# Out-projection begun with three of four head pairs, and roundings reordered around the turned rows, in a two-block transformer kernel

## The chip, the cores and the metric

One core of one Trainium2 chip runs the whole program. The metric is the device time of one execution in microseconds; lower is better. TensorE is called PE here, ScalarE ACT, VectorE DVE, GpSimd POOL and SyncE SP, as in the profile.

## The reference

The input is 256 tokens of width 1024 in float32. Two blocks of two layers each are computed one after the other.

First block, per layer: `h = rms_norm(x)`; `z = h @ w_in` (2560 columns); three mixers read z; their outputs are concatenated and `x = x + mix @ w_out`; then an MLP.

```
o_att = block_attention(rope(norm(q_a)), rope(norm(k_a)), v_a)      # 8 heads of 64, 2 kv heads
o_hg  = hgrn2_bidirectional(...)                                   # 4 heads, gated recurrence both ways
o_cv  = silu(layer_norm(depthwise_conv(a * sigmoid(gate)) + b_dw)) # 256 channels, 31 taps
x = x + concat([o_att, o_hg, o_cv]) @ w_out
x = x + square(relu(rms_norm(x) @ w_mlp_in)) @ w_mlp_out
```

Second block: layer 0 is a gated linear attention, layer 1 a dilated attention of 3 groups and 6 slots over shared keys; both have 4 more heads over an outside memory. Then `x = layer_norm(alpha * x + mix @ w_out)` and `x = layer_norm(alpha * x + peer(x))`, where `peer` picks 16 of 16384 experts for each of 8 heads and is computed densely, with a table of gates.

## The kernel before, in words

**Products in three parts.** Every float32 operand of a large product is split into a high part, rounded to the format fp32r, and a low part, the rest. One product is three matmuls (L1630, L1631, L1632 in `three`): high x high, low x high, high x low. The weights come as 403 panels of 128 x 2048 (1 MB) in one stream. SP loads a panel into one of 4 slots `RAW`; ACT rounds it (`hi`, L468); DVE subtracts (`lo`, L992), POOL for a few of them; PE multiplies. `hi_to(n)` and `lo_to(n)` do this for all panels up to n, so the place of such a call in ACT's or DVE's program sets what stands behind the rounding. The semaphores are `raw_loaded`, `hi_ready`, `lo_ready` and `hp_used` (PE is done with the panel). SP reloads a slot on `lo_ready`. A panel's result is in one of four PSUM banks `PS` (lin in the trace); the reader frees it through `bank_free`. The other four banks are `M`.

**Order.** Each engine runs its own list of instructions, written out by hand; they meet only in semaphores.

**Start.** ACT loads constants, `LBS` (lower bounds) and `PR` (parameters). DVE waits for all three (`cst_loaded` at 48), shifts `LBS` (L1037 to L1039), ACT takes the exponential (L511), DVE finishes (L1041 to L1051). Only behind L511 does ACT take the squares of the rows of x in `rms_rows` (L503); DVE scales the rows (`norm_rows`, L1021); PE turns them (`transposes`, L1617). Ahead of the turns PE runs copies of constants into a bank that nobody reads (`warm`, L1607): 11 at the start, 2 at later norms. ACT rounds the turned rows into `XH` (`xh_evict`, L481), DVE makes `XL` (`xl_evict`, L1007), and the first panel's products can begin.

**Norms between layers.** `rms_rows` begins when DVE has added all four quarters of the panel products to x (`residual`, L1031). In layer 1 of the first block ACT then rounds two panels (`hi_to(h0 + 3)`) before `xh_evict`. Meanwhile PE multiplies a panel of the memory's keys and values (`mem_panel`).

**Mixers and out-projection of the first block.** `eight_heads_act` and `eight_heads_dve` carry the softmax of the 8 heads, in four pairs; the convolution's taps (L1826) run on PE in between. ACT writes the pairs' outputs into `MIXF[0:4]` (`out_`, L411); the recurrence is in `MIXF[4:6]` early, the convolution in `MIXF[6:8]` last. ACT rounds `MIXF[0:4]` in one piece (L586), DVE subtracts (`mix_low`, L1146). DVE copies the taps out (L1165, four pieces), PE sums over channels (`over_channels`, L1835), and waits for `mixl_ready`. Then come the four out-projection panels (`wide`): panels 0 and 1 take k = 0 to 3 (the heads), in the order 2, 3, 0, 1, for both tiles of 128 tokens; panels 2 and 3 take k = 4 to 7. Between the tiles of panel 0 PE sums the squares of the channels (`variance`), which DVE has made in four steps (L1172, L1173). ACT and DVE finish the convolution's layer norm and gate; `MIXF[4:8]` is rounded in one piece (L593).

**Second block.** In layer 0 ACT rounds a panel (`hi_to(s0 + 3)`) and then copies the turned rows. In its gated attention the four memory heads run between the last panels: on ACT `squares(0)`, `exps(0)`, `squares(1)`, `exps(1)` and so on; on DVE `head_max(0)`, `head_max(1)`, one panel's low part (`lo_to(s0 + 10)`), `head_scale(0)`; PE then turns head 0 (L2036) and later multiplies it with the values (L2046), behind ACT's copy (L721). In layer 1 `mixing_panel(u)` on ACT first rounds the panel u + 3 and then copies out the result of panel u (L671), for which PE's `slot_scores` (L2106) wait; the out-projection's first half (`out_half`) waits for the high and low part of four slots (L761, L1344).

## Time and profile before

| | us |
|---|---|
| median of 3 runs | 2624.73 |
| lowest, highest | 2624.46, 2628.49 |
| the profiled execution, its own time | 2624.61 |
| its span in the trace | 2622.8 |
| PE busy | 2567.4 |
| DVE busy | 1689.8 |
| ACT busy | 1324.9 |

The trace is one execution. Its times count from the span's start. A line of the timeline gives start, duration, engine, line of the kernel, operation, the tile written and those read, the shape, the number of merged instructions, and in brackets the idle time before and who ended it. Matmuls are pipelined, so the durations of neighbours overlap. Line numbers are those of the kernel before. A line of the table of stretches gives the stretch, its length, busy us (and instructions) of PE, PEld (weight loads), DVE, ACT and POOL, then the granted clock of PE as a share of 2.4 GHz, the DMA engines' share and GB/s.

### The profile page before, as it was taken

What the parts mean: (1) busy time and instruction counts of PE and PEld (TensorE: products, weight loads), DVE (VectorE), ACT (ScalarE), POOL (GpSimd) and SP (SyncE); (2) the same over time, 40 slices, a digit from 0 to 9 for tenths busy, and PEclk for the clock granted to TensorE, in tenths of its full rate; (3) what the DMA queues carried; (4) which work ended last, traced back from release to release, by engine and by line L of the source; (5) the groups of instructions that cost most, each with busy time, mean ns of one, the idle gap of its engine ahead of it and who ended that gap; (6) DMA issues with size and microseconds to landing.
All of it is one profiled execution on the core that took longest, in us unless ns stands there. A gap on an engine that the chain in (4) does not pass through costs nothing.

```text
span 2622.8 us, 45628 instructions
## 1 busy us (share of the span) xinstructions
PE 2567.4 (98%) x18648; PEld 2341.1 (89%) x18648; DVE 1689.8 (64%) x2677; ACT 1324.9 (51%) x1587; POOL 163.0 (6%) x74
## 2 busy tenths in 40 slices
PE   8999999999999999999999999989999999999998
PEld 7889898798889999999999887978999999999887
DVE  5766457664456999655555666577999555555666
ACT  4455343554364679544444444444678544444443
POOL 0000000000004500000000000003500000000000
PEclk9999999999999999999999999999999999999999
DMA  6245552355526456855656675524456765656672
GB/s 246 95 180 193 192 209 101 124 215 195 195 87 231 146 208 225 289 216 217 218 214 216 232 272 192 210 84 166 152 199 225 293 224 209 221 211 222 230 272 104
DMA packets 75007, 520.14 MB, mean 198 GB/s; under 512 B 8352, under 2 KB 8624, under 8 KB 18928
## 3 DMA queue, kind: packets, MB, share of 16 engines
q1 hardware_dynamic: 58592, 424.70, 44.6%
q0 software_dynamic: 10208, 43.45, 4.8%
q10 hardware_dynamic: 6064, 49.97, 4.6%
q8 instruction: 103, 1.69, 0.3%
q14 instruction: 40, 0.33, 0.0%
HBM read 478.25 MB, written 39.85 MB: 198 GB/s over the span
## 4 chain that ended last, share of the span: by engine, by line
PE 88%; DVE 9%; ACT 1%; issue 1%; DMA 0%; ACTq 0%; DVEq 0%
PE lin L1630 17%; PE lin L1632 17%; PE lin L1631 17%; PE m L1631 9%; PE m L1630 9%; PE m L1632 9%; PE m L2249 4%; DVE lo L992 1%; PE m L1764 1%; PE lin L1826 1%; PE m L1785 1%; PE m L2223 0%; ACT hi L468 0%; PE m L2106 0%; PE m L1797 0%
## 5 line engine op out<-in xcount | busy, mean ns | idle before, releaser
L992 DVE TENSOR_TENSOR lo<-raw,hi 128x2048 fp32r<-128x2048 f32 x351 | 802.5, 2291 | 635.6 <-ACT hi L468 634.5
L468 ACT ACTIVATE hi<-raw 128x2048 fp32r<-128x2048 f32 x403 | 769.9, 1913 | 456.3 <-PE m L1632 331.8
L1630 PE MATMUL lin<-xh,hi 128*128 128x256 f32 x3344 | 943.4, 282 | 8.1 <-DVE lo L992 4.6
L1631 PE MATMUL lin<-xl,hi 128*128 128x256 f32 x3344 | 925.0, 277 | 0.0
L1632 PE MATMUL lin<-xh,lo 128*128 128x256 f32 x3344 | 924.9, 277 | 0.0
L1630 PEld LDWEIGHTS lin<-xh,hi 128*128 128x128 f32 x3344 | 628.1, 188 | 15.8 <-issue 6.8
L1631 PEld LDWEIGHTS lin<-xl,hi 128*128 128x128 f32 x3344 | 628.5, 188 | 3.7 <-issue 1.0
L1632 PEld LDWEIGHTS lin<-xh,lo 128*128 128x128 f32 x3344 | 628.0, 188 | 0.0
L1630 PE MATMUL m<-hi,ah 128*128 128x512 f32 x1024 | 398.8, 389 | 0.0
L1631 PE MATMUL m<-lo,ah 128*128 128x512 f32 x1024 | 398.8, 389 | 0.0
L1632 PE MATMUL m<-hi,al 128*128 128x512 f32 x1024 | 398.6, 389 | 0.0
L851 ACT ACTIVATE h<-lin 128x512 f32<-128x512 f32 x128 | 76.2, 595 | 318.3 <-PE lin L1632 296.0
L1632 PEld LDWEIGHTS m<-hi,al 128*128 128x128 f32 x1024 | 192.2, 188 | 40.0
L1630 PEld LDWEIGHTS m<-hi,ah 128*128 128x128 f32 x1024 | 192.2, 188 | 38.5 <-DVE al L1503 0.8
L1631 PEld LDWEIGHTS m<-lo,ah 128*128 128x128 f32 x1024 | 192.2, 188 | 37.7
L1587 POOL TENSOR_TENSOR lo<-raw,hi 128x2048 fp32r<-128x2048 f32 x27 | 124.2, 4612 | 235.3 <-DVE lo L992 205.7
L2249 PE MATMUL m<-ob,oa 128*128 128x128 f32 x1024 | 135.2, 275 | 0.0
L1630 PE MATMUL lin<-hi,xh 128*128 128x256 f32 (+2 forms) x368 | 121.0, 329 | 6.8 <-DVE xl L1015 2.1
L2249 PEld LDWEIGHTS m<-ob,oa 128*128 128x128 f32 x1024 | 124.3, 191 | 1.2 <-issue 0.3
L1632 PE MATMUL lin<-hi,xl 128*128 128x256 f32 (+2 forms) x368 | 117.8, 320 | 0.0
L1631 PE MATMUL lin<-lo,xh 128*128 128x256 f32 (+2 forms) x368 | 117.4, 319 | 0.0
L1593 POOL DMA_DIRECT2D g<-gate_table x32 | 28.3, 886 | 1328.1 <-DVE h L1498 972.4
(355 smaller groups left out, 2769.4 us busy)
## 6 DMA issues: line engine op xcount, KB each, us to landing
raw<-stream SPq DMA_DIRECT2D x403, 1024.0 KB, 4.8
gate_table<-stg ACTq DMA_DIRECT2D x16, 2048.0 KB, 10.7
g<-gate_table POOLq DMA_DIRECT2D x32, 1024.0 KB, 8.0
rows<-rows ACTq DMA_DIRECT2D x4, 1024.0 KB, 6.8
memh<-mem_turned_scratch POOLq DMA_DIRECT2D x3, 1024.0 KB, 5.1
meml<-mem_turned_scratch POOLq DMA_DIRECT2D x3, 1024.0 KB, 8.3
dg<-taps ACTq DMA_DIRECT2D x2, 1152.0 KB, 9.6
x_scratch<-x ACTq DMA_DIRECT2D x2, 1024.0 KB, 4.2
```

The costliest lines, as they stand in the source:

```text
L468: act.activation(HI[i % SLOTS][:], RAW[:, i % SLOTS, :], ACT.Copy).then_inc(hi_ready, 1)
L851: act.activation(H[:, s % AHEAD, :], PS[s % 4][:], ACT.Gelu).then_inc(sem("ge_ready"), 1)
L992: dve.tensor_tensor(low_part(i), RAW[:, i % SLOTS, :], HI[i % SLOTS][:].bitcast(F32), ALU.subtract).then_inc(lo_ready, 1)
L1587: pool.tensor_tensor(low_part(i), RAW[:, i % SLOTS, :], HI[i % SLOTS][:].bitcast(F32), ALU.subtract).then_inc(lo_ready, 1)
L1593: pool.dma_start(G[c % 2][:].rearrange("p g b t -> p g (b t)"), tab[l][:, :, GB * STORE * c:GB * STORE * c + GB * STORE].rearrange("g a x ...
L1630: pe.matmul(out_, ah, bh, start=first, stop=False, **kw)
L1631: pe.matmul(out_, ah, bl, start=False, stop=False, **kw)
L1632: return pe.matmul(out_, al, bh, start=False, stop=last, **kw)
L1764: last[j] = pe.matmul(to[:, 64 * tt:64 * tt + 64].rearrange("p (b m) -> p b m", m=m), KS[o, d, t], halves(QS[o, d, t], m)[:, :, 1 - d, :], ...
L1785: last[j] = pe.matmul(halves(M[3][o, c + P * tt:c + P * tt + P], m)[:, :, 1 - d, :], VR[:, tt, 64 * h:64 * h + 64], sc[:, 64 * tt:64 * tt ...
L1826: ins = pe.matmul(CV[r][o:o + 64, 0:256], taps_i, UP[p, ct, i:i + TOK], start=(i == 0), stop=(i == CONV_K - 1), skip_group_check=True)
L2249: ins = pe.matmul(M[k % 4][:, KEYS * t:KEYS * t + KEYS], oa[:, t, :], ob[:, t, :], start=True, stop=True)
```

## The change

- Start: `rms_rows` no longer waits for the lower bounds. The whole work on them becomes a function `lower_bounds()` on DVE, called behind `lo_to(3)`; ACT's exponential stands behind `hi_to(h0 + 3)`, ahead of the fourth panel's rounding. 5 warm-up copies in place of 11.
- `rms_rows` with a second argument waits per tile: for the two quarters of tile 0, then its squares, then those of tile 1.
- Layer 1 of the first block: `hi_to(h0 + 2)` before the copies of turned rows, `hi_to(h0 + 3)` behind them. Second block, layer 0: `xh_evict(4)` before `hi_to(s0 + 3)`.
- Out-projection of the first block: `MIXF` is rounded as 0:3, 3:4, 4:6 and 6:8. PE begins panel 0 with k = 0, 1, 2, then sums over channels, then k = 3; it sums the squares behind k = 1 of the second tile. Panels 2 and 3 take k in two parts, (0, 1) for both tiles and then (2, 3). `mixl_ready` counts 4 per layer.
- Gated attention: `exps(1)` before `squares(1)` on ACT, `lo_to(s0 + 10)` before `head_max(0)` on DVE.
- Last layer: for the panels 6 to 9 of `mixing_panel` the rounding stands behind the copy.

The diff, cut to its core:

```
@@ eight_heads_act
                 if p < 2:
                     exps(2 * p + 4)
+            first_pairs()
             out_(3)
@@ scalar
-            def rms_rows(junk):
+            def rms_rows(junk, added=None):
                 for tt in range(TT):
+                    for n in range(2 if added is not None else 0):
+                        evicted(act, added + 2 * n + tt)
                     a.step(act.activation(junk[:, tt, :], X[:, tt, :], ACT.Square, accum_out=SMALL[:, tt:tt + 1]))
...
-            act.wait_ge(sem("lb_shifted"), 1)
-            a.step(act.activation(LBS[:, 0:8], LBS[:, 0:8], ACT.Exp), sem("lb_exp"))
...
-                    for u in range(4):
-                        evicted(act, h0 - 5 + u)
-                rms_rows(XS)
+                    rms_rows(XS, h0 - 5)
+                else:
+                    rms_rows(XS)
...
-                    hi_to(h0 + 3)
+                    hi_to(h0 + 2)
                     act.wait_ge(hp_used, h0)
                 xh_evict(2 * l, lambda k: par(l, "norm_mix", k))
+                hi_to(h0 + 3)
                 if l == 0:
                     hi_to(h0 + 3)
+                    act.wait_ge(sem("lb_shifted"), 1)
+                    a.step(act.activation(LBS[:, 0:8], LBS[:, 0:8], ACT.Exp), sem("lb_exp"))
...
+                def mix_high(a0, a1):
+                    a.mark(act.activation(flat(XH[:, a0:a1, :]), flat(MIXF[:, a0:a1, :]), ACT.Copy), sem("mixh_ready"))
+
+                def first_pairs():
+                    act.wait_ge(sem("o_ready"), 8 * l + 6)
+                    mix_high(0, 3)
+
+                eight_heads_act(act, a, l, gates, first_pairs)
                 act.wait_ge(sem("o_ready"), 8 * l + 8)
-                a.mark(act.activation(flat(XH[:, 0:4, :]), flat(MIXF[:, 0:4, :]), ACT.Copy), sem("mixh_ready"))
+                mix_high(3, 4)
+                act.wait_ge(sem("recurrent_ready"), l + 1)
+                mix_high(4, 6)
...
-                a.mark(act.activation(flat(XH[:, 4:8, :]), flat(MIXF[:, 4:8, :]), ACT.Copy), sem("mixh_ready"))
+                mix_high(6, 8)
...
-                for u in range(4):
-                    evicted(act, h1 - 5 + u)
-                rms_rows(XS2)
+                rms_rows(XS2, h1 - 5)
...
                 if l == 0:
+                    xh_evict(4)
                     hi_to(s0 + 3)
-                    xh_evict(4)
...
-                    hi_to(s0 + u + 4)
+                    late = l == 1 and u >= MEM_H + 2
+                    if not late:
+                        hi_to(s0 + u + 4)
...
                     ins.then_inc(bank_free[i % 4], 1)
+                    if late:
+                        hi_to(s0 + u + 4)
...
                     exps(0)
+                    exps(1)
                     squares(1)
-                    exps(1)
@@ vector
-            dve.wait_ge(sem("cst_loaded"), 48)
...
                 if l == 0:
                     lo_to(1)
+                    dve.wait_ge(sem("cst_loaded"), 48)
                 xl_evict(2 * l, lambda k: par(l, "norm_mix", k))
+                if l == 0:
+                    lo_to(3)
+                    lower_bounds()
                 lo_to(h0 + 6)
...
                 lo_to(h0 + N_IN + N_OUT - 1)
+                mix_low(0, 3, 4 * l + 1)
...
-                mix_low(0, 4, 2 * l + 1)
+                mix_low(3, 4, 4 * l + 2)
...
+                mix_low(4, 6, 4 * l + 3)
                 lo_to(h0 + N_IN + N_OUT)
...
-                mix_low(4, 8, 2 * l + 2)
+                mix_low(6, 8, 4 * l + 4)
...
+                    lo_to(s0 + 10)
                     head_max(0)
                     head_max(1)
-                    lo_to(s0 + 10)
@@ tensor
-                transposes(2 * l, XS, lambda: pe.wait_ge(sem("rows_ready"), 2 * l + 1), 11 if l == 0 else 2)
+                transposes(2 * l, XS, lambda: pe.wait_ge(sem("rows_ready"), 2 * l + 1), 5 if l == 0 else 2)
...
-                over_channels(("cy0_ready", 4), AC, M[0], "csum_done")
-                pe.wait_ge(sem("mixl_ready"), 2 * l + 1)
+                pe.wait_ge(sem("mixl_ready"), 4 * l + 1)
...
-                        pe.wait_ge(sem("mixl_ready"), 2 * l + 2)
+                        pe.wait_ge(sem("mixl_ready"), 4 * l + 3)
...
+                    def channel_sums(tt, k):
+                        if (u, tt, k) == (0, 0, 2):
+                            over_channels(("cy0_ready", 4), AC, M[0], "csum_done")
+                            pe.wait_ge(sem("mixl_ready"), 4 * l + 2)
+                        elif (u, tt, k) == (0, 1, 1):
                             over_channels(("csq_ready", 2), EG, M[1], "cvar_done")
+                        elif (u, tt, k) == (2, 1, 1):
+                            pe.wait_ge(sem("mixl_ready"), 4 * l + 4)
...
+                    wide(h0 + N_IN + u, h0 + N_IN, u % 2, XH, XL, 4 * (u // 2), u < 2, u >= 2, between=channel_sums,
+                         parts=((0, 1, 2, 3),) if u < 2 else ((0, 1), (2, 3)))
```

## Rows read from the trace of the kernel before

**Rows 1.** The page's first part: busy us (share of the span) xinstructions.

```profile
PE 2567.4 (98%) x18648; PEld 2341.1 (89%) x18648; DVE 1689.8 (64%) x2677; ACT 1324.9 (51%) x1587; POOL 163.0 (6%) x74
```

**Rows 2.** PE's waits: tile, line, whom it waited for; us in total, times, longest.

```profile
PE m L1835 <- DVE ac L1165: 2.1, 2, 1.0
```

**Rows 3.** Timeline of the first 21 us; columns as in the section above.

```profile
10.94 6.94 PE L1607 MATMUL m<-cst 128*128 128x256 f32 x22 [10.94 <-DMA pr<-par]
10.94 4.35 PE L1607 MATMUL m<-cst 128*128 128x256 f32 x10 [10.94 <-DMA pr<-par]
...
8.31 0.70 POOL L1562 DMA_DIRECT2D lev<-lev  x1 [7.86 <-DMA x<-x]
...
17.71 1.91 PE L1617 MATMUL m<-cst,xs 128*128 128x128 f32 x16
...
20.25 0.36 PE L1630 MATMUL lin<-hi,xh 128*128 128x256 f32 x1 [0.62 <-DVE xl L1007]
```

**Rows 4.** Timeline, 354 to 361 us, the norm of layer 1.

```profile
354.87 3.71 ACT L468 ACTIVATE hi<-raw 128x2048 fp32r<-128x2048 f32 x2
...
357.05 1.91 PE L1617 MATMUL m<-cst,xs 128*128 128x128 f32 x16
...
360.37 0.35 PE L1630 MATMUL lin<-hi,xh 128*128 128x256 f32 x1 [1.41 <-DVE xl L1007]
```

**Rows 5.** Timeline, 134 to 145 us, the out-projection of layer 0.

```profile
134.50 1.09 ACT L407 ACTIVATE pt<-lin 128x512 f32<-128x512 f32 x2
...
139.22 1.06 ACT L586 ACTIVATE xh<-mixf 128x1024 fp32r<-128x1024 f32 x1
139.71 1.13 PE L1835 MATMUL m<-ac,cst 128*128 128x256 f32 x4 [1.05 <-DVE ac L1165]
140.37 1.23 DVE L1146 TENSOR_TENSOR xl<-mixf,xh 128x1024 fp32r<-128x1024 f32 x1 [0.72 <-ACT xh L586]
141.63 0.42 DVE L1172 SCALAR_TENSOR_TENSOR w<-m,ac 128x256 f32<-128x256 f32 x1
141.66 0.50 PE L1630 MATMUL lin<-hi,xh 128*128 128x512 f32 x1 [0.81 <-DVE xl L1146]
...
144.53 1.02 PE L1835 MATMUL m<-eg,cst 128*128 128x256 f32 x4
```

**Rows 6.** Timeline, 693 to 697 us, the start of the second block.

```profile
693.39 1.91 ACT L468 ACTIVATE hi<-raw 128x2048 fp32r<-128x2048 f32 x1 [12.40 <-issue]
...
696.65 0.36 PE L1630 MATMUL lin<-xh,hi 128*128 128x256 f32 x1 [1.08 <-DVE xl L1004]
```

**Rows 7.** Timeline, 757 to 767 us, the gated attention's memory heads.

```profile
757.22 2.29 DVE L992 TENSOR_TENSOR lo<-raw,hi 128x2048 fp32r<-128x2048 f32 x1
...
760.38 0.63 PE L2036 MATMUL m<-cst,pm 128*128 128x128 f32 x4 [2.02 <-DVE pm L1306]
...
763.37 0.60 ACT L721 ACTIVATE pt<-m 128x512 f32<-128x512 f32 x1
...
766.56 1.08 PE L2046 MATMUL m<-pt,kvl 128*64 128x256 f32 x4
```

**Rows 8.** Stretches with busy times, granted clock; ahead, the second fall's idle.

```profile
1635.64 1.49 PE L1625 MATMUL m<-cst,x 128*128 128x128 f32 x8 [2.05 <-DVE x L1225]
...
762.00:766.00 4.00, 4.00 (x22) 4.00 (x22) 3.72 (x6) 3.97 (x10) 0.00 (x0) 0.57 0.45 188
1636.00:1640.00 4.00, 4.00 (x17) 3.46 (x16) 3.76 (x7) 2.99 (x3) 4.00 (x1) 0.57 0.00 0
```

**Rows 9.** Timeline, 1754 to 1768 us, the last layer's slots.

```profile
1754.42 0.89 PE L2106 MATMUL m<-kd,qd 128*128 128x256 f32 x3 [1.40 <-ACT qd L671]
...
1765.55 0.83 ACT L761 ACTIVATE xh<-mix 128x768 fp32r<-128x768 f32 x1
1765.80 1.53 PE L2106 MATMUL m<-kd,qd 128*128 128x256 f32 x6 [1.71 <-ACT qd L671]
...
1767.76 0.50 PE L1630 MATMUL lin<-hi,xh 128*128 128x512 f32 x1 [0.44 <-DVE xl L1344]
```

More of the change, by code:

```diff
@@ L1048, in _, with lower_bounds @@
-            for l in range(DEPTH):
-                v.step(dve.tensor_tensor(lb4[l], p4[l], p4[0], ALU.subtract))
-                v.step(dve.tensor_scalar(LB[:, l, :, :, 1], lb4[l], -1.0, 1.0, ALU.mult, ALU.add))
-            dve.memset(UP[:], 0.0).then_inc(sem("hid_ready"), 2)
+            def lower_bounds():
+                v.step(dve.tensor_tensor(LBS[:, 8:12], LBS[:, 0:4], LBS[:, 4:8], ALU.max))
+                v.step(dve.tensor_tensor(LBS[:, 0:4], LBS[:, 0:4], LBS[:, 8:12], ALU.subtract))
+                v.step(dve.tensor_tensor(LBS[:, 4:8], LBS[:, 4:8], LBS[:, 8:12], ALU.subtract), sem("lb_shifted"))
+                dve.wait_ge(sem("lb_exp"), 1)
+                v.step(dve.tensor_tensor(LBS[:, 8:12], LBS[:, 0:4], LBS[:, 4:8], ALU.add))
+                v.step(dve.reciprocal(LBS[:, 8:12], LBS[:, 8:12]))
+                v.step(dve.tensor_tensor(LBS[:, 0:4], LBS[:, 0:4], LBS[:, 8:12], ALU.mult))
+                v.step(dve.tensor_tensor(LBS[:, 4:8], LBS[:, 4:8], LBS[:, 8:12], ALU.mult))
+                v.step(dve.tensor_tensor(LBS[:, 4:8], LBS[:, 4:8], LBS[:, 0:4], ALU.add))
+                lb4 = [LB[:, l, :, :, 0].rearrange("p a b -> p a b") for l in range(DEPTH)]
+                p4 = [LBS[:, 4 * l:4 * l + 4].rearrange("p (a b) -> p a b", b=2) for l in range(DEPTH)]
+                for l in range(DEPTH):
+                    v.step(dve.tensor_tensor(lb4[l], p4[l], p4[0], ALU.subtract))
+                    v.step(dve.tensor_scalar(LB[:, l, :, :, 1], lb4[l], -1.0, 1.0, ALU.mult, ALU.add))
+                dve.memset(UP[:], 0.0).then_inc(sem("hid_ready"), 2)
@@ L1574, in _ @@
                 elif g == 2:
-                    pool.wait_ge(sem("mixl_ready"), 4)
+                    pool.wait_ge(sem("mixl_ready"), 8)
                 else:
@@ L1688, in row_half, with wide @@
                     ins.then_inc(hp_used, 1)
-            def wide(i, i0, n, hh, hl, k0, first, last, between=lambda tt: None):
+            def wide(i, i0, n, hh, hl, k0, first, last, between=lambda tt, k: None, parts=((2, 3, 0, 1),)):
                 pe.wait_ge(lo_ready, i + 1)
                 wh, wl = (t.rearrange("p (k n) -> p k n", k=KT // 2) for t in (HI[i % SLOTS][:], low_part(i)))
-                for tt in range(TT):
-                    j = i0 + 2 * n + tt
-                    if first and reads_before(j) > 0:
-                        pe.wait_ge(bank_free[j % 4], reads_before(j))
-                    for k in (2, 3, 0, 1):
-                        ins = three(PS[j % 4][:], hh[:, k0 + k, P * tt:P * tt + P], hl[:, k0 + k, P * tt:P * tt + P], wh[:, k, :], wl[:, k, :],
-                                    first and k == 2, last and k == 1, skip_group_check=True)
-                    if tt == 0:
-                        between(tt)
+                for ks in parts:
+                    for tt in range(TT):
+                        j = i0 + 2 * n + tt
+                        if first and ks == parts[0] and reads_before(j) > 0:
+                            pe.wait_ge(bank_free[j % 4], reads_before(j))
+                        for k in ks:
+                            ins = three(PS[j % 4][:], hh[:, k0 + k, P * tt:P * tt + P], hl[:, k0 + k, P * tt:P * tt + P], wh[:, k, :], wl[:, k, :],
+                                        first and k == parts[0][0], last and k == parts[-1][-1], skip_group_check=True)
+                            between(tt, k)
                 ins.then_inc(hp_used, 1)
```

19 lines of the change are left out of this document (2 added, 17 removed).

## The prediction

> **What bounds the kernel now.** The page comes first: TensorE (PE) is busy for 98% of the span [rows 1], and the profiled execution's own time, 2624.61 us, is the span of 2622.8 and 1.8 around it, 0.1 below the median of the runs. So the change can win only where PE idles, where PE does padding, or where its clock is low. The second view is the list of PE's waits, 22 lines; the longest by far, 10.94 us, is the first loads [rows 3], which the change leaves alone. The rest are idles of 0.4 to 2.0 us, and most are handovers: PE has finished, ScalarE (ACT) or VectorE (DVE) has just begun to round the next operand into high and low part. The third view is the timeline around each idle that the diff touches; there one reads which instruction sits ahead of the one that PE waits for. The fourth is the table of stretches with the granted clock. An idle that sits behind work which can stand elsewhere goes; an idle that is the plain latency of copy and subtraction stays.
>
> **A, the start.** ACT's squares wait today for three DVE steps and an exponential on the lower bounds, and these for the last parameter load, which also releases PE at 10.94 [rows 3]; they begin at 11.75. Afterwards the squares need x alone, and x has landed by 8.3, when POOL, which waits for it, issues its load [rows 3]. The four steps of the row norm then end near 11.1 and the scaled rows are there near 12.5. PE does not notice before its warm-up copies are done, of which 12 of 22 records go (11 copies become 5, two records each). 22 take 6.94 us and 10 take 4.35 [rows 3], so the transposes begin 2.6 us earlier, near 15.1. Behind them stands the same chain (transposes at 17.71, first product at 20.25 [rows 3]), and the first panel's parts are ready: rounding from 11.1, 1.9 + 2.3 us, so by 15.5. The lower bounds come back behind the third panel's subtraction: 12 small DVE steps and a clear, some 3 us, and ACT waits for the first three of them with the fourth panel's rounding queued behind it. That rounding ends near 28 and its subtraction near 31, and PE wants it near 34 (first product at 17.7, three panels of 5.4 us). The cover is 3 us; if it were gone the wait would be about 1 us. Gain 2.6; bounds 1.0 (the second panel's rows land late) and 5.1 (12 records at the low rate of the first ten, 0.43 us each).
>
> **B, the norm by tiles, and the rounding behind the copies.** In layer 1 of the first block two roundings of 1.9 us stand on ACT between the row norm and the copies of the turned rows: they begin at 354.87 and last 3.71, to 358.58, though the transposes began at 357.05 [rows 4]. One of them moves behind. At the start of the kernel, where nothing stands in between, PE's first product comes 2.54 after the transposes' beginning [rows 3]; here 3.32 [rows 4]. Gain 0.8. The tile-wise order of the squares adds nothing: PE reaches the transposes by its own work (padding copies end at 357.05), and the same holds at the two MLP norms. The moved rounding ends near 362.5 and is wanted two panels later, 370. Bounds 0.5 and 1.4, the whole idle.
>
> **C, the out-projection, twice.** PE idles 1.05 before the channel sums, because the taps are copied out, and 0.8 after them, because the rounding of eight heads has only begun [rows 2, 5]. Now three pairs are rounded early: ACT is free at 135.6 and takes 0.83 for 768 columns [rows 5, 9], DVE three quarters of 1.23 [rows 5], so the low part is there at 137.4, before PE is free at 138.66 (139.71 less 1.05). PE runs nine products of the first panel, then the sums (their input is ready at 139.7), then k = 3 on the fourth pair, whose parts need 0.4 + 0.4 after 139.2 and are ready near 140.2. Both idles go, 1.86 us. New is the wait for the squares before the second sums: between the two sums PE now has 9 products where it had none beside an idle and 12; 12 took 2.87 (141.66 to 144.53 [rows 5]), so 9 take about 2.1. DVE needs four steps of 0.42 with gaps of 0.04, 1.85, and about 0.3 of handover: I take 0.2 of idle, with 0 and 0.5 as ends. The last part, channels 6 to 8, is ready some 14 us after the panel's start and wanted after 15.5, since the third panel now does (0, 1) for both tiles first. Gain 1.7 each, 3.3 together (2.7 to 3.8).
>
> Cutting two roundings into four costs engine time: 768 columns take 0.83 and 1024 take 1.06 [rows 5, 9], so a quarter costs 0.23 as part of a long one and 0.42 alone; the four pieces cost ACT and DVE about 0.3 each per layer, at a place where both idle for microseconds. The Trainium skill (VectorE: DVE Perf Modes, the section on the TRN2 errata) speaks against this edit: each instruction with an SBUF source pays a fixed extra, so one should keep tiles at 512 elements or more. The rows agree in direction, but the sum would only change if the pieces lay on PE's path; I put them in at nothing.
>
> **D, the second block's first layer.** At its start one rounding, 693.39 to 695.30, stands ahead of the copies of turned rows, and PE idles 1.08 [rows 6]. It moves behind; the copies begin at 693.4, the first low part is there at 694.7, while PE's padding runs to 695.57 (696.65 less 1.08). The whole 1.08 goes (0.9 to 1.1).
>
> In the gated attention PE idles 2.02 before the first turn of the memory heads: DVE starts a 2.29 us subtraction at 757.22 just as the first exponentials end, and scales the head only behind it [rows 7]. That subtraction moves ahead of the maxima, into more than 10 us of DVE idle. The scale then ends near 758.3, when PE is free (758.36). Close behind that idle the granted clock falls: its mean over the 4 us from 762 is 0.57 [rows 8], that is, it lies for the most part at the 1.2 GHz level, and 4 x 0.43 = 1.7 us of work are lost. Yet not all 3.7 can be had: the next value product needs ACT's copy of the turned head, which ends at 763.97 [rows 7], and ACT only swaps its second exponentials with four squares, so that this time stays. PE would be there at 763.0 and waits 1.0. The value product began at 766.56 [rows 7], now 764.0: gain 2.5 (2.0 if the low stretch comes all the same, 3.7 if ACT is quicker). Behind it ACT and DVE follow PE.
>
> **E, late roundings in the last layer.** PE idles 1.40 at 1754.42 and 1.71 at 1765.80, both for an eviction that stands behind a rounding of 1.8 us [rows 9]. With the eviction first, the first idle goes (ACT is free at 1752.0, PE done with the panel at 1752.2, evicted by 1752.9, wanted at 1753.0). The second goes too, but behind it stands the out-projection's first half, which needs four slots in both parts. ACT does the same things in another order, evict, round, round 768 columns, copy, round 256, and DVE subtracts last. So that half starts when it did, at 1767.76 [rows 9], or 0.1 to 0.2 later, now behind one idle of about 2.2 us in place of 1.71 and 0.44. Gain 1.4 - 0.15 = 1.25 (1.0 to 3.0).
>
> **The clock.** Before the granted clock fell at 762 PE had idled 2.02 us [rows 7]; it falls once more, at 1636, to the same mean of 0.57 [rows 8], and there too PE had just idled, for 2.05 [rows 8]. Behind the idles of 1.4 and 1.7 [rows 9] it stays at the 2.4 GHz level. The new idle of 2.2 us resembles the first two, so I charge E one low stretch, 1.7 us; with none the charge is 0.
>
> Sum: 2.6 + 0.8 + 3.3 + 1.1 + 2.5 + 1.25 = 11.55, less 1.7, is 9.85: 2624.6 - 9.9 = 2614.7 us.
>
> **Rivals.** (1) Everything as above, but the new 2.2 us idle brings no low stretch: 2613.0. For it: two cases are few. Against: they are all the cases there are. (2) The handover takes the place of the waits: in C the squares are late by the full 0.5 and the third panel waits for the last channels, A gives 1.0 only because the second panel's rows land late, and E's second idle grows. Then A 1.0, B 0.5, C 2.0, D 3.0, E 1.0, less 1.7, a gain of 5.8: 2618.8. For it: in all these places the margin is under 1 us. (3) The change does not do what it says in the large term: the clock falls elsewhere, because idles between 1.0 and 1.7 us now meet other work, once or twice (1.7 each) more than charged, so 9.9 less 3.4 to 5.1 leaves 4.8 to 6.5: 2620. (4) Slower: the five copies left do not bring PE's clock up. Today the rate rises within the first ten records, so this has the row against it; but if it stayed at 1.2 GHz behind the shorter warm-up, every 2 us at that level would cost 1, and the gain of 9.9 is eaten when the low level lasts 20 us beyond the transposes, four panels. At eight panels, 5.4 us more each for the last four, it would be near 2636.
>
> **How the numbers follow.** Forecast 0.42; rival 1 0.27; rival 2 0.15; rival 3 0.13, of which half ends within 0.2%; rival 4 0.03. Of rival 2 I put 0.02 within 0.2%. A difference of 0.2%, 5.2 us, is about what a measurement of this kernel can tell from no change. Faster by more: 0.42 + 0.27 + 0.13 + 0.07 = 0.89. Within: 0.02 + 0.06 = 0.08. Slower: 0.03. The range reaches from a little under rival 1 (its upper ends in A and D, 2611) to rival 2 and the near end of rival 3 (2619.5).
>
> **What would show it.** In the changed kernel's timeline: first product of panel 0 near 17.7; no idle before the channel sums or after them, and at most 0.5 before the second sums; the idle before the memory heads' first turn gone, no low clock behind it, and an idle of about 1.0 before the first value product; first product of the second block straight behind the padding; one idle of about 2.2 before the last layer's out-projection, with or without a low granted clock behind it. PE's waits should sum to 7 or 8 us less. The forecast is wrong if the first 20 us show no shift, if either out-projection shows a new wait in its third panel, or if more than two low stretches stand in the table.

## The result, and the profile after

| us | before | after |
|---|---|---|
| median of 5 runs each | 2625.16 | 2611.55 |
| lowest, highest | 2624.46, 2628.49 | 2611.21, 2613.14 |
| the profiled execution, its own time | 2624.61 | 2611.21 |
| its span | 2622.8 | 2608.7 |

The ratio is 0.9946, with a 95% interval of 0.9934 to 0.9958: faster by 13.6 us, where the forecast had 9.9. The time is inside the range (2611.0 to 2619.5), close to its lower end, and below the forecast and every rival; as a gain, 13.6 is the very most that the range allowed (2624.6 less 2611.0). By the bound of 0.2% it is faster, as said with 0.89.

The span of the profiled execution shrank by 14.1 us and its time by 13.4, because the time outside the span is 1.8 us before and 2.5 after. No run shows why. The parts below are read in the span.

The first section of the page of the changed kernel (busy us, share, instructions) answers to [rows 1]. PE is busy for 6.4 us less; the other 7.7 of the 14.1 us of span are waits, 7 or 8 in the forecast.

```profile
PE 2561.0 (98%) x18636; PEld 2336.0 (90%) x18636; DVE 1689.4 (65%) x2681; ACT 1325.3 (51%) x1591; POOL 163.1 (6%) x74
```

Timeline of PE in the changed kernel, the places of the prediction in their order (start, duration, engine, line, operation, tiles, shape, merged count, idle before and its releaser). L1650 is the first of the three matmuls of a product, L1855 the sum over channels, L2071 the memory heads' value product, L1645 the turning by tiles:

```profile
10.88 4.43 PE L1627 MATMUL m<-cst 128*128 128x256 f32 x10 [10.88 <-DMA pr<-par]
17.75 0.36 PE L1650 MATMUL lin<-hi,xh 128*128 128x256 f32 x1 [0.69 <-DVE xl L1021]
...
138.40 1.02 PE L1855 MATMUL m<-ac,cst 128*128 128x256 f32 x4
...
141.40 1.13 PE L1855 MATMUL m<-eg,cst 128*128 128x256 f32 x4
...
171.11 0.36 PE L1650 MATMUL lin<-xh,hi 128*128 128x256 f32 x1 [0.62 <-DVE xl L1021]
...
355.22 0.36 PE L1650 MATMUL lin<-hi,xh 128*128 128x256 f32 x1 [0.68 <-DVE xl L1021]
...
684.24 1.97 PE L1637 MATMUL m<-cst,x 128*128 128x128 f32 x16 [1.60 <-DVE small L1265]
...
688.01 0.47 PE L1650 MATMUL lin<-xh,hi 128*128 128x256 f32 x1
...
755.58 1.08 PE L2071 MATMUL m<-pt,kvl 128*64 128x256 f32 x4 [0.99 <-ACT pt L735]
...
809.93 0.36 PE L1650 MATMUL lin<-xh,hi 128*128 128x256 f32 x1 [1.50 <-DVE xl L1029]
...
1624.64 1.09 PE L1645 MATMUL m<-cst,x 128*128 128x128 f32 x8 [1.76 <-DVE x L1245]
...
1753.59 0.50 PE L1650 MATMUL lin<-hi,xh 128*128 128x512 f32 x1 [2.23 <-DVE xl L1364]
```

The first product of panel 0 is at 17.75 ([rows 3] had 20.25). Neither sum over channels has an idle in front ([rows 5] had 1.05, and 0.8 behind the first). The norm of layer 1 has 0.68 in place of 1.41 [rows 4]. The second block's first product has no idle in brackets ([rows 6] had 1.08). The 2.02 before the memory heads' first turn is gone and 0.99 stands before the value product [rows 7]. One idle of 2.23 stands before the last out-projection where 1.40, 1.71 and 0.44 stood [rows 9]. Each of these was forecast.

Table of stretches of the changed kernel, at the places of [rows 8] and behind the new 2.23 (busy us of PE, PEld, DVE, ACT, POOL with instruction counts, then the granted clock, DMA share, GB/s). The clock is at 1.00, the 2.4 GHz level, in all three, where the two stretches of [rows 8] had 0.57. In the changed kernel's trace it falls only in the last 3 us of the program, as it does at the end of every execution here; that last fall is left out below:

```profile
755.00:759.00 4.00, 3.42 (x18) 2.32 (x19) 1.28 (x4) 3.33 (x10) 0.00 (x0) 1.00 0.66 233
1624.00:1628.00 4.00, 3.35 (x24) 3.11 (x25) 3.90 (x7) 3.02 (x4) 3.56 (x1) 1.00 0.04 14
1753.00:1757.00 4.00, 3.41 (x15) 2.85 (x16) 3.83 (x10) 1.03 (x2) 0.00 (x0) 1.00 0.67 252
```

Laid beside the kernel before, start by start, the two timelines give what each part was worth in this pair of executions:

| part | forecast | measured | from |
|---|---|---|---|
| A, start | 2.6 | 2.50 | 20.25 to 17.75 |
| B, norm of layer 1 | 0.8 | 0.77 | shift 4.38 (MLP norm of layer 0) to 5.15 (355.22) |
| C, out-projection, two layers | 3.3 | 4.06 | shifts 2.38 to 4.38, and 5.16 to 7.22 |
| D, second block's start | 1.1 | 1.35 | shift 7.21 (turning at 684.24) to 8.56 (729.17) |
| D, gated attention | 2.5 | 2.42 | shift 8.56 to 10.98 (755.58) |
| norm near 809 | 0 | -0.34 | shift 10.98 to 10.64; idle 1.50, 1.14 before |
| idle near 1624 | 0 | 0.36 | shift 10.64 to 11.00 (1624.64); idle 1.76, 2.05 before |
| the low stretch behind it | 0 | 1.72 | shift 11.00 to 12.72 (1667.43) |
| E, last layer | 1.25 | 1.45 | shift 12.72 to 14.17 (1753.59) |
| E, a low stretch behind 2.23 | -1.7 | 0 | clock 1.00 in 1753 to 1757 |
| sum | 9.85 | 14.2 | the parts, less 0.1 of scatter between them; span 14.1 less |

The mechanisms of A to E are all there. Of the 4.3 us missed in the span (3.7 in the time), 3.4 are the clock, and most of the rest is C.

### The profile page after: what moved, and what is told of

The parts are those of the page before. It is cut to its first block, busy times and chain, and to the rows that moved or that the text cites. A ratio compares the mean times of both kernels' runs of the same rounds, so it can differ in the third digit from the quotient of the medians.

```text
span 2608.7 us, 45616 instructions
## 1 busy us (share of the span) xinstructions
PE 2561.0 (98%) x18636; PEld 2336.0 (90%) x18636; DVE 1689.4 (65%) x2681; ACT 1325.3 (51%) x1591; POOL 163.1 (6%) x74
## 4 chain that ended last, share of the span: by engine, by line
PE 89%; DVE 9%; ACT 1%; issue 1%; DMA 0%; ACTq 0%; DVEq 0%
PE lin L1650 17%; PE lin L1652 17%; PE lin L1651 17%; PE m L1651 9%; PE m L1650 9%; PE m L1652 9%; PE m L2274 4%; DVE lo L1006 1%; PE m L1784 1%; PE lin L1846 1%; PE m L1805 1%; PE m L2248 0%; PE m L2131 0%; PE m L1817 0%; DVE eq L1481 0%
## 5 line engine op out<-in xcount | busy, mean ns | idle before, releaser
L1650 PE MATMUL lin<-xh,hi 128*128 128x256 f32 x3344 | 943.7, 282 | 7.4 <-DVE lo L1006 4.6
L1650 PEld LDWEIGHTS lin<-xh,hi 128*128 128x128 f32 x3344 | 628.3, 188 | 14.8 <-issue 5.7
L1650 PE MATMUL m<-hi,ah 128*128 128x512 f32 x1024 | 398.9, 390 | 0.0
L1650 PEld LDWEIGHTS m<-hi,ah 128*128 128x128 f32 x1024 | 192.2, 188 | 38.6 <-DVE al L1523 0.8
L1650 PE MATMUL lin<-hi,xh 128*128 128x256 f32 (+2 forms) x368 | 120.1, 326 | 6.3 <-DVE xl L1364 2.2
```

Source lines behind the costliest of these rows:

```text
L1650: pe.matmul(out_, ah, bh, start=first, stop=False, **kw)
```

## The experiments

A low stretch is a time in which the granted clock is at the 1.2 GHz level; a single one and a double one, twice as long, occur. There are three theories of what brings it. L, mine from the prediction: an idle of 2.0 or more is followed by a low stretch. M: it matters when the idle falls. R: low stretches come in one execution of a program and not in the next. From the fifth run on, M takes R in: the moment is a thing that differs between executions. Shifts below are against the kernel before (its second execution and the four runs with one part alone) or the changed kernel (the others), always between two points of the same timelines, so that the start, which varies, drops out. The runs went to three chips; chip alone does not tell them apart, since on the one where five of six profiled executions had no low stretch, nine timed executions of the kernel before had mean granted clocks of 0.996 to 0.998.

### The kernel before once more

> The kernel before, unchanged, in a second profiled execution. It asks what the two low-clock stretches behind the idles of 2.02 us (near 762) and 2.05 us (near 1636) are. Theory L (the length of the idle decides): both stand again, with a mean granted clock of about 0.57 over four microseconds, and the span is 2622.8 within 0.5. Theory M (it matters when the idle falls): in an execution with the same instruction times both stand again too, at the same places. Theory R (they come in one execution and not in the next): one or both are missing, 1.7 us off the span for each, or stand elsewhere.

No edit. Span 2626.6, 3.8 more. Stretches with the granted clock:

```profile
142.00:146.00 4.00, 3.58 (x9) 2.83 (x10) 3.83 (x6) 0.00 (x0) 0.00 (x0) 0.57 0.00 0
764.00:771.00 7.00, 7.00 (x29) 5.89 (x29) 3.84 (x6) 4.48 (x10) 0.00 (x0) 0.53 0.46 173
1641.00:1645.00 4.00, 4.00 (x19) 3.64 (x18) 3.90 (x6) 2.53 (x4) 2.92 (x1) 0.58 0.00 0
```

Both stretches stand again, as L and M say, but the one behind 2.02 lasts twice as long, and a third has come behind the pair of idles 1.04 and 0.81 of the out-projection, which had none behind it in the first execution. So one execution does not show what the next will have, as R says, and length alone is refuted as the rule. M as first put (same places again) is wrong too; but everything came 0.6 us later here (first product at 20.89, 20.25 before), so the moments were not the same.

### The gated attention alone

```
+                    exps(1)
                     squares(1)
-                    exps(1)
...
+                    lo_to(s0 + 10)
                     head_max(0)
                     head_max(1)
-                    lo_to(s0 + 10)
```

> The kernel before with the gated attention's two moves alone: one subtraction of VectorE ahead of the head maxima, and the second exponentials ahead of the second squares on ScalarE. My theory, as forecast: the idle of 2.0 before the memory heads' first turn goes, one of 1.0 before the first value product comes, and that product is 2.5 earlier; the low stretch near 762 is gone with the idle, which is what makes 1.7 of the gain's cover, and the one at 1636 (now 1633.5) stays, so the span is 2622.8 - 2.5 - (0 to 0.2) = 2620.2. Theory M (it matters when the idle falls): the idle near 1636 falls 2.5 us earlier by the clock and its low stretch may be gone, then 2618.5. The rival that the moved subtraction delays the maxima gives 2621 or more.

From 739.85 to the value product at 766.24 it is 26.39, and 28.83 in the kernel before (737.73 to 766.56): 2.44, as forecast, with one idle of 0.88 before the value product. The idle near 1636 is 1.76 here, not 2.05, though the edit is 870 us away, and no low stretch follows it:

```profile
1635.33 1.09 PE L1625 MATMUL m<-cst,x 128*128 128x128 f32 x8 [1.76 <-DVE x L1225]
```

One follows the pair 1.05 and 0.81 of layer 1's out-projection (granted clock 0.57 in 483 to 487), which theory L does not foresee. Span 2621.1. The gated attention's term of part D is confirmed.

### The last layer alone

```
-                    hi_to(s0 + u + 4)
+                    late = l == 1 and u >= MEM_H + 2
+                    if not late:
+                        hi_to(s0 + u + 4)
...
+                    if late:
+                        hi_to(s0 + u + 4)
```

> The kernel before with the late roundings of the last layer alone. Everything up to 1750 is as before. My theory, as forecast: idles of 1.40 and 1.71 + 0.44 become one of 2.2 before the out-projection's first half, which begins 1.4 earlier (1766.3). Theory L (the length decides, above about 2.0): a low stretch follows that idle and costs 1.7, so the span is 2622.8 - 1.4 + 1.7 = 2623.1. Theory M (not the length but when it falls): none, as in the changed kernel, 2621.4; the stretches at 762 and 1636 stand as before in both.

```profile
1769.24 0.50 PE L1634 MATMUL lin<-hi,xh 128*128 128x512 f32 x1 [2.23 <-DVE xl L1348]
```

```profile
1769.00:1773.00 4.00, 3.76 (x17) 3.14 (x18) 3.49 (x9) 1.03 (x2) 0.00 (x0) 1.00 0.62 246
```

PE's timeline and the table of stretches: the same idle of 2.23, no low clock behind it. From 1683.05 the first half comes 86.19 later, 87.61 before: 1.42, E's gain alone. The span of 2624.3 is longer than before's for two reasons that have nothing to do with the edit: a double low stretch near 762, and 1.4 us at the second block's start, where ACT's issue of the DMA for `WG2` took 1.91 in place of 0.45 and stood in front of its copies; the idle there was 2.46, and no low stretch followed. Behind the new idle L is wrong; the span that M gave is missed by the two accidents.

### The out-projection alone

Edit: the hunks of `mix_high`, `mix_low`, `wide` and `channel_sums` of the diff, nothing else.

> The kernel before with the out-projection's part alone (three pairs first, four pieces, sums between products). The changed kernel showed 2.0 to 2.1 per layer where I had 1.7. Theory of the forecast, corrected: 2.0 per layer also when it stands alone, 4.1 by the first product of layer 1's MLP. The rival, that part of the 2.0 belongs to the tile-wise norm behind the out-projection, gives 1.7 here and 0.3 missing. Clock: the idles near 762 and 1636 keep their length (2.02 and 2.05) but come 4.1 us earlier; theory L keeps both low stretches (span 2618.7), theory M may lose one or both (2617.0 or 2615.3).

From the head scores to the MLP's first product it is 62.97 in layer 0 and 61.21 in layer 1, 64.99 and 63.28 before: 2.02 and 2.07, no idle before either sum. So the 2.0 per layer is the out-projection's own. There is no low stretch in the whole execution, though the idle before the memory heads' turn was as long as ever. The other idle did not keep its length as expected: near 1631 it is 1.76, as with the gated attention alone. Span 2616.4. PE's timeline, and the stretch behind:

```profile
756.79 0.63 PE L2053 MATMUL m<-cst,pm 128*128 128x128 f32 x4 [2.12 <-DVE pm L1318]
```

```profile
757.00:761.00 4.00, 4.00 (x30) 3.44 (x29) 2.35 (x3) 3.99 (x7) 0.00 (x0) 1.00 0.74 264
```

This run also prices the clock. The stretch from the first product with `qtd` (L1984) to the value product is the same work in executions with the same gated attention: 27.39 here and 27.20 in the run with the second block's start alone, both without a low stretch; 28.83 before with a single one; 30.35 in the second execution of before (740.18 to 770.53) and 30.50 in the run with the last layer alone, both with a double one. A single one costs 1.4 to 1.6 here, and 1.70 near 1636 (44.51 and 42.81 from the turning to L1711, with and without).

### The changed kernel once more, and with other warm-ups

The first has no edit. The second:

```
-                transposes(2 * l, XS, lambda: pe.wait_ge(sem("rows_ready"), 2 * l + 1), 5 if l == 0 else 2)
+                transposes(2 * l, XS, lambda: pe.wait_ge(sem("rows_ready"), 2 * l + 1), 11 if l == 0 else 2)
```

The third has a 2 there.

> The changed kernel, unchanged, in a second profiled execution. The first had no low-clock stretch, though PE idled 1.76 near 1623 and 2.23 near 1751; in four executions of the kernel before and of parts of it, low stretches stood behind idles of 2.0 to 2.1 in some and not in others, and behind a pair of 1.05 and 0.81 in two. Theory M (it matters when an idle falls, and this differs from one execution to the next): one low stretch or none, 0 to 1.7 us, span 2608.7 to 2610.5, and where the stretch comes need not be the longest idle. Rival: the changed kernel is free of them by its shape: none, 2608.7 within 0.3. The idle before the first product behind the tile-wise norm near 809 (1.50 here, 1.14 in all others) tells whether that 0.36 belongs to the change: if yes 1.5 again, if it was this execution's own, 1.14.

> The changed kernel with the eleven padding copies at the start put back; the input norm stays first. Forecast's theory of part A: the gain at the start is the dropped copies alone, so the first product of panel 0 is 2.5 later than in the changed kernel, at 20.2, and everything behind it moves by as much: span 2611.2. Rival: the earlier norm has a share of its own (the transposes wait for the rows as well), then the first product comes before 20.0. All later idles fall 2.5 us later at the same length: theory M lets a low stretch come (up to 3.4 us more, 2614.6), the rival that the shape decides gives none.

> The changed kernel with two padding copies at the start in place of five. In the changed kernel the scaled rows are there at 12.2, the first panel's low part at 15.1, the transposes begin at 15.14, and the granted clock rises at 14.9. My theory: the transposes begin near 12.7 at the lower rate and end near 15, the first product comes at 15.3 to 16.0, 1.8 to 2.4 earlier, and the clock is up by then; span 2606.3 to 2607. The rival of the prediction, that a shorter warm-up leaves the clock low: the first product is earlier as well, but the products behind it take twice as long for some microseconds, and the span is 2609 or more.

The unchanged one: span 2607.8, no low stretch, 2.23 and 1.76 idle again, 1.49 near 809. With 11 copies: first product at 20.57, span 2611.6, 2.9 more, and again no low stretch with all idles 3 us later. With 2 copies: first product at 16.12, span 2607.3, a little later than the 15.3 to 16.0 and 2606.3 to 2607 expected. PE's timeline at its start:

```profile
10.91 2.07 PE L1627 MATMUL m<-cst 128*128 128x256 f32 x4 [10.91 <-DMA pr<-par]
12.78 2.52 PE L1637 MATMUL m<-cst,xs 128*128 128x128 f32 x16
16.12 0.36 PE L1650 MATMUL lin<-hi,xh 128*128 128x256 f32 x1 [0.82 <-DVE xl L1021]
```

The turns themselves now do the warming: they take 2.52 in place of 1.91, since the first are spaced 0.21 and those from 14.04 on 0.11, and the products behind them run at their full rate, 0.12 apart. Rival 4 of the prediction, that a shorter warm-up leaves the clock low, is refuted down to two copies. With 11 copies the earlier norm brings nothing that the start's scatter does not hide. With 5 it is needed: in the kernel before, the first low part is ready only at 18.81, so 5 copies with the old norm would gain at most 1.4 of the 2.5 (an estimate from the row below; that combination was not run).

```profile
16.52 2.29 DVE L992 TENSOR_TENSOR lo<-raw,hi 128x2048 fp32r<-128x2048 f32 x1 [0.53 <-ACT hi L468]
```

That the three spans do not differ by round numbers is the start's own scatter: the first ten records of copies took 4.43, 3.87 and 4.62 us in the three executions that have them. The Trainium skill (TensorE: Matmul & The Clock Gate, Part 1) says that the number of slow matmuls at a kernel's start differs from run to run of one kernel. The trace agrees: all ten records are spaced over 0.4 us in the changed kernel's first execution, the first seven in its second. Six executions with 11 copies and the old norm begin at 19.81 to 20.89 (mean 20.5), five with 5 copies at 17.25 to 18.47 (mean 17.75), so A is worth 2.75 on average.

### The last layer's order

Behind panel 9 no rounding follows the copy any more; it stands behind the fourth slot's.

```
-                    if late:
+                    if late and u < MEM_H + 5:
                         hi_to(s0 + u + 4)
...
                             mix_high(sl, sl + 1)
+                        if sl == SLOT_H - 3:
+                            hi_to(s0 + p1 + sl + 4)
...
-                    weights = {4: o, 6: o + 1, 8: o + 2, 10: o + 3, 11: o + N_OUT}
+                    weights = {4: o, 6: o + 1, 9: o + 2, 10: o + 3, 11: o + N_OUT}
```

> The changed kernel with the last layer's two weight steps moved once more: ScalarE's rounding behind panel 9 goes behind both roundings of the slots, VectorE's subtraction behind the tenth slot sum. Theory: the 2.23 idle before the out-projection's first half is the sum of these two in front of it (1.8 on ScalarE, then the slots' subtractions), so it shrinks to 0.3 to 0.6, the first half begins at 1751.9 in place of 1753.6, and 1.7 us are gained; with no low stretch near, the span is 2607.0. Rival: the work put off comes back, as a wait for the second half's low part or for the next scores, then the gain at 1784 (first product of the query panels) is under 1.0.

PE's timeline, and a stretch of the table:

```profile
1752.65 0.50 PE L1652 MATMUL lin<-hi,xh 128*128 128x512 f32 x1 [0.51 <-DVE xl L1366]
...
1765.50 0.66 PE L2146 MATMUL m<-cst,pd 128*128 128x128 f32 x4 [1.67 <-DVE pd L1390]
```

```profile
1784.00:1788.00 4.00, 3.21 (x15) 3.24 (x16) 3.90 (x7) 1.50 (x4) 0.00 (x0) 0.57 0.02 4
```

The first half comes 46.51 behind the slot scores at 1706.14, 48.27 in the changed kernel: 1.76 gained. But the wait before the last turn grows from 0.45 to 1.67, because VectorE subtracts a panel between its last two slot sums, and 0.55 is left at the next panels: the rival. A low stretch stands at 1784, at idles of 1.11 and 1.07, and costs 1.4; span 2610.3.

### How much room the squares have

```
                 mix_low(3, 4, 4 * l + 2)
+                mix_low(4, 6, 4 * l + 3)
                 dve.wait_ge(sem("csum_done"), l + 1)
...
-                mix_low(4, 6, 4 * l + 3)
                 lo_to(h0 + N_IN + N_OUT)
```

> The changed kernel with VectorE's subtraction of channels 4 to 6 (one instruction of 0.69) ahead of the four steps that make the squares, in both layers' out-projections. It tests why the idle of 0.2 that I had expected before the second sums did not come. Theory: in the changed kernel the squares are ready at 141.34 and the second sums begin at 141.40, just in time; 0.69 to 0.74 more on VectorE then opens an idle of 0.6 to 0.7 before the second sums of each layer, and the first product of the MLP comes that much later, 1.3 together, span 2610.0. Rival: there is slack of 0.5 or more, because PE reaches the second sums later than I read: no idle, span 2608.7 within 0.4.

The first attempt measured nothing: the instruction fell into the 1.7 us in which DVE waits for the sums, and sums to sums stayed at 3.00 (137.78 to 140.78). The rival's outcome, no idle, came out, but for another reason than the rival's; the span was 2607.9. So the same instruction went behind the wait:

```
                 dve.wait_ge(sem("csum_done"), l + 1)
+                mix_low(4, 6, 4 * l + 3)
                 for ct in range(2):
```

> The changed kernel with the same subtraction of 0.69 on VectorE moved to stand behind its wait for the first sums, directly ahead of the squares. In the run before this one it sat ahead of that wait, where VectorE idled for 1.7, and moved nothing. Theory: first sums to second sums are 3.00 in the changed kernel (138.40 to 141.40), the squares are ready 0.06 before; with 0.74 more on VectorE the second sums begin 0.7 later, in both layers, 1.4 together, span 2609.2 to 2610.2. Rival: PE has a slack of half a microsecond that the view hides (the ends of products are modelled): 0.2 or less per layer.

PE's timeline (both sums of layer 0, the last layer's first half), and the stretch behind the last of them:

```profile
138.69 1.02 PE L1855 MATMUL m<-ac,cst 128*128 128x256 f32 x4
142.40 1.13 PE L1855 MATMUL m<-eg,cst 128*128 128x256 f32 x4 [0.61 <-DVE eg L1193]
...
1755.15 0.50 PE L1650 MATMUL lin<-hi,xh 128*128 128x512 f32 x1 [2.23 <-DVE xl L1364]
```

```profile
1755.00:1759.00 4.00, 3.85 (x11) 3.10 (x12) 3.40 (x9) 1.03 (x2) 0.00 (x0) 0.65 0.54 229
```

3.71 in place of 3.00, in both layers: of 0.74 added, 0.71 arrive. The squares are on the path with a margin of 0.03 to 0.06. And here, for the only time in seven executions, a low stretch follows the idle of 2.23.

### The second block's start alone

```
                 if l == 0:
+                    xh_evict(4)
                     hi_to(s0 + 3)
-                    xh_evict(4)
```

> The kernel before with one thing changed: at the second block's start the copies of the turned rows go ahead of the third weight rounding. Forecast: the whole idle of 1.08 goes. The changed kernel showed 1.4 between the beginning of the transposes and the first product (5.20 and 3.77). Theory: 1.4 here too, since the first product then starts under the end of the last padding copy, which is modelled; the rival, that 0.3 of it comes from another part, gives 1.1. Second question: the idle before the norm's product near 820 (1.14 in the kernel before and three partial ones, 1.50 in every execution of the changed kernel): 1.50 here would place it in this move, 1.14 in the start or the norms. Clock: theory M says nothing of which idle is followed by a low stretch; span 2621.4 or 1.7 to 3.4 on either side.

693.88 (turning) to 738.81 is 44.93; 46.28 before; 1.35, as in the changed kernel. The idle near 820 is 1.14, so this move does not bring the 1.50. Both idles of 2.0 are there and neither has a low stretch behind it; one stands behind 1.04 and 0.81 in layer 0's out-projection. Span 2621.0.

### Taken further

```
                 if l == 0:
+                    xh_evict(4)
...
                     act.dma_start(dst_, src_).then_inc(sem(f"mix_loaded{l}"), 16)
...
-                    warm(5, PS[3])
+                    warm(1, PS[3])
...
+                    turned(0)
                     mixing_panel(8)
-                    turned(0)
...
-                    weights = {4: o, 6: o + 1, 8: o + 2, 10: o + 3, 11: o + N_OUT}
+                    weights = {4: o, 6: o + 1, 9: o + 2, 11: o + N_OUT}
```

The copies of the turned rows go ahead of the four DMA issues; the start has two copies, and the last layer the rounding of the run with the new order.

> The changed kernel taken further by what the traces showed, four places, each read by its own milestone. (a) Two padding copies at the start: first product at 16.1, 1.6 earlier. (b) At the second block's start ScalarE copies the turned rows ahead of its four DMA issues (1.8 us) and the padding behind the transposes shrinks from five copies to one: the first product comes 2.0 behind the transposes' beginning in place of 3.77, a gain of 1.4 to 1.8; rival: the first low part waits for VectorE and an idle of 0.5 or more remains, gain 1.0. (c) In the gated attention the copy of the turned head goes ahead of the panel's rounding: the 0.98 before the first value product goes, gain 0.9 to 1.0; rival: it comes back at the next turn. (d) In the last layer, as in the run before but with VectorE's subtraction for the third panel behind the last slot sum: out-projection's first half 1.75 earlier, and the idle before the last turn 0.5 in place of 1.67, gain 1.6 to 1.75. Sum 5.5 to 6.1: span 2603.0, time 2605.5; a low-clock stretch in some of the executions adds 1.7. Theory of the rivals: 3.5, 2607.5.

Median of 5 runs 2604.37 (2604.18 to 2606.07); ratio to the kernel before 0.9916 (0.9903 to 0.9930). That kernel was timed again beside it, nine times: median 2627.06, 2624.10 to 2631.03, so 1.9 more than in the section on the result; against the 2625.16 there the ratio would be 0.9921. Against the changed kernel the span of the profiled execution is 6.3 shorter, 2602.4: (a) 1.56; (b) 1.60 (682.76 to 726.09 is 43.33, 44.93 there); (c) 0.81 by the norm near 806 (1.07 at the value product, less a new 0.18 before the next turn and what follows); (d) 2.44 by the query panels (1.74 at the first half, and the wait before the last turn gone too). In the expectation (d) was too small by 0.7, (c) too large by 0.1 to 0.2. No low stretch. PE's timeline:

```profile
682.76 1.97 PE L1640 MATMUL m<-cst,x 128*128 128x128 f32 x16 [1.60 <-DVE small L1268]
684.57 0.60 PE L1630 MATMUL lin<-cst 128*128 128x256 f32 x2
685.00 0.36 PE L1653 MATMUL lin<-xh,hi 128*128 128x256 f32 x1
...
1748.00 0.51 PE L1653 MATMUL lin<-hi,xh 128*128 128x512 f32 x1 [0.51 <-DVE xl L1367]
```

At the second block's start the padding had hidden a wait: in the changed kernel ten records of copies, 2.3 us, covered what four DMA issues on ScalarE cost (0.34 to 0.61 each there), and no idle showed.

## Why the prediction was off

**The clock, 3.4 of 4.3 us, is the step that failed.** The prediction said of the two low stretches "two cases are few" and "they are all the cases there are", took the one at 1636 as fixed, and charged a third behind the new 2.2 us idle. All fourteen profiled executions together hold 17 idles of 2.0 us or more on PE (the first loads aside); a low stretch follows 7 of them: 3 of 5 before the memory heads' turn, 3 of 4 near 1636, 1 of 7 before the last out-projection, and not the 2.46 at the second block's start. Four more follow pairs of idles of 0.8 to 1.1 us that stand 1 us apart. Two identical executions of before had 2 stretches and 4 (a double one counted as two). So a row that shows a low stretch once does not show that the next execution has it. Theory L, by which length is enough, falls. M, that it is the moment of the idle, contradicts none of the fourteen, but no run set a moment on purpose, so it is argued and not shown.

R alone, a pure draw, does not fit either, for the program sets how often a low stretch can come. None of the 58 idles between 1.5 and 2.0 us in the fourteen executions has one behind it. The idle near 1636 is 2.04 or 2.05 in four executions, three of them with a low stretch, and 1.76 or 1.77 in the other ten (both of the changed kernel, its six variants, and the runs with the gated attention or the out-projection alone), none with one. The change also took away the idle before the memory heads' turn and the out-projection's pairs. Little is left: the changed kernel's two profiled executions have no low stretch and its six variants have two together, where the kernel before has 2 in one execution and 3 in the other (the double one counted once). The timed executions say the same: the mean granted clock, 0.998 for the execution with two low stretches and 0.999 or more for those with one or none, is 0.996 to 0.998 in all fourteen executions of the kernel before that list it, and 0.999 or 1.000 in all six of the changed kernel. So the 1.7 us at 1636 went together with an idle that had become 0.29 shorter, which the prediction put at nothing; why it became shorter no run shows. The 1.7 us charged behind the new 2.2 us idle are the draw that came once in seven.

Reckoned without the clock: the span of the kernel before less its two stretches (1.44 and 1.70 by the comparisons above) is 2619.7; the changed one 2608.7; the difference 11.0. The forecast's own terms without the clock are 11.55 less the 1.7 that part D counted for the stretch near 762, 9.85. There the miss is 1.1.

**C, 0.76 too small.** I took 0.2 of idle per layer before the second sums and there is none. The estimate had 9 products at 2.1 against 1.85 and 0.3 of VectorE; in the trace PE takes 2.33 from 139.07 to 141.40, since the first product behind the sums is spaced 0.42 where its neighbours have 0.23, and the squares are ready at 141.34. The run with 0.71 of 0.74 arriving shows how close that is. The other 0.15 per layer lies in how an idle is read: a product that need not wait begins under the end of its predecessor (the sums at 138.40 begin 0.16 before the modelled end of the product at 138.17), so taking a wait away gives the wait and the overlap.

**D's start, 0.25 too small, and E, 0.2,** for the same reason: 1.35 with a wait of 1.08. A product that waited started 0.1 to 0.3 later against the work before it than one that did not.

**What held:** A (2.5 for 2.6), B (0.77 for 0.8), the gated attention (2.42 for 2.5, with the 1.0 before the value product that keeps the whole 3.7 from being had), the single idle of 2.2 in the last layer, the out-projection's later parts (no wait in the third panel). The moved lower bounds and the cut roundings cost nothing on PE's path, as put in.

**Rivals.** Rival 1, no low stretch behind the 2.2 us idle, was the right branch; at 2613.0 it was still too long by the stretch at 1636. Rival 2 was wrong at each of its places: squares, third panel, second rows. Rival 3 had the right suspicion, clock that falls elsewhere, and only one sign for it; its sum was wrong too, since one or two low stretches more than charged are 1.7 to 3.4 us, not 3.4 to 5.1, which leaves gains of 6.5 to 8.2. Rival 4 is refuted by the run with two copies; its 2636 does not follow from its terms either, for four panels of 5.4 us each take twice 20 us at the lower rate, and not 20.

**Open.** The idle near 809 is 1.49 or 1.50 in the changed kernel, twice, and in five of its variants; it is 1.13 or 1.14 in the kernel before, in the four partial ones and, unexpectedly, in the variant with one VectorE subtraction moved behind the first sums, 300 us earlier and more. In the timeline VectorE starts 0.46 behind ScalarE's first copy in place of 0.10, with nothing else recorded on it. It follows the program and not the execution, like the 1.76 or 2.05 near 1636; no run shows the cause of either.

## What to carry to other kernels

A low-clock stretch behind an idle of about 2 us is one draw from several: look at a second execution before you charge or credit one, and weight its price by how often it came (7 of 17 idles here). The same idle 0.3 us shorter had none in ten executions: compare the lengths in every execution, also where the edit does not reach. Count what a removed wait brings as the wait and 0.1 to 0.3 us of overlap on top. Padding that ends just as the next operand arrives hides a wait that no view lists: look at what the producer did in that time, its DMA issues too.

## What the runs showed of the hardware

The granted clock of one program differs between executions: 2 single stretches at the 1.2 GHz level in one, 2 single and a double one in the next, none in the changed kernel in two; each single one cost 1.4 to 1.7 us. A low stretch followed 7 of 17 idles of 2.0 to 2.5 us and none of 58 of 1.5 to 2.0. The first ten records of padding copies took 3.9 to 4.6 us with these copies unchanged, and with five copies the first product came at 17.25 to 18.47. One DMA issue on ScalarE took 1.91 us in one execution and 0.45 in the thirteen others.
